# Three edits to a two-layer hybrid encoder trunk: narrow products as columns of the value product, the scatter inside the next item's gate projection, the dense down projection by pairs of blocks

## The reference, cut to what matters

```
FOX_COLS = (FOX_W, FOX_W, FOX_W, FOX_HEADS)                       # 256, 256, 256, 4
DSA_COLS = (DSA_W, DSA_KV_RANK, IDX_HEADS * IDX_HEAD_DIM, IDX_HEAD_DIM, IDX_HEADS)  # 256, 128, 256, 32, 8

rel = relu(einsum('bqhd,bkd->bqhk', qi, k_idx))                   # the one key serves all 8 indexer heads
score = einsum('bqhk,bqh->bqk', rel, wi) * idx_scale

def swiglu(h, w_gate, w_up, w_down):
    return (silu(h @ w_gate) * (h @ w_up)) @ w_down

y = zeros_like(h)                                                 # layer 1: experts
for e in range(N_EXPERTS):
    y = y + gates[..., e:e + 1] * swiglu(h, w_gate[e], w_up[e], w_down[e])
x = x + y
```

## Time and profile before

| what | us |
|---|---|
| three runs: median | 1974.56 |
| lowest, highest | 1971.77, 1974.73 |
| the profiled execution | 1971.14 |
| its span, first to last instruction | 1969.4 |

### The profile page before, as it was taken

One profiled execution on the slowest core, in us unless ns is written; L12 is line 12 of the kernel. 1 busy time (PEld: TensorE's weight loads), 2 busy tenths in 40 slices (PEclk: granted clock), 3 DMA queues, 4 the chain that ended last, 5 costly groups with the idle time before them and its releaser, 6 DMA issues.

```text
span 1969.4 us, 42199 instructions
## 1 busy us (share of the span) xinstructions
PE 1889.3 (96%) x19476; PEld 1260.9 (64%) x19476; DVE 360.0 (18%) x757; ACT 261.4 (13%) x502; POOL 54.1 (3%) x108
## 2 busy tenths in 40 slices
PE   7999999999998999999799999999999999999996
PEld 6887888788887887888635446354453534545364
DVE  1256223100001356223300101001010010100102
ACT  1224111100001324111100000000001000010001
POOL 2100200000000000200000000000000000000000
PEclk9999999999999999999699999999999999999998
DMA  6432212443434332112699999999999999999970
GB/s 182 139 139 86 85 47 86 171 157 142 141 106 136 123 129 86 66 66 86 278 339 366 379 368 393 350 369 363 364 399 362 364 359 361 391 372 374 354 285 23
DMA packets 120758, 462.08 MB, mean 235 GB/s; under 512 B 7486, under 2 KB 18416, under 8 KB 104208
## 3 DMA queue, kind: packets, MB, share of 16 engines
q1 hardware_dynamic: 120592, 459.46, 62.0%
HBM read 458.39 MB, written 1.05 MB: 233 GB/s over the span
## 4 chain that ended last, share of the span: by engine, by line
PE 95%; DVE 2%; ACT 1%; issue 1%; DMA 1%; SPq 0%; DVEq 0%; ACTq 0%
PE bank L989 29%; PE bank L381 25%; PE bank L1013 15%; PE bank L892 4%; PE bank L682 3%; PE bank L852 3%; PE bank L963 2%; PE bank L723 2%; PE bank L839 1%; PE bank L1063 1%; PE bank L1000 1%; PE bank L394 1%; PE bank L367 1%; DMA slot<-in_ffn_w_gate 0%; PE bank L766 0%
## 5 line engine op out<-in xcount | busy, mean ns | idle before, releaser
L989 PE MATMUL bank<-slot,xg 128*32 128x512 f32 (+1 forms) x6144 | 580.6, 539 | 0.7 <-DVE xg L2090 0.7
L381 PE MATMUL bank<-h,slot 128*128 128x256 f32 x2176 | 486.5, 383 | 6.5 <-ACT rel L1442 4.4
L381 PEld LDWEIGHTS bank<-h,slot 128*128 128x128 f32 x2176 | 413.8, 192 | 69.6 <-issue 12.7
L989 PEld LDWEIGHTS bank<-slot,xg 128*32 128x32 f32 x6144 | 207.8, 110 | 367.1 <-issue 355.4
L1013 PE MATMUL bank<-slot,aT 128*32 128x256 f32 x5376 | 295.2, 379 | 0.0
L1013 PEld LDWEIGHTS bank<-slot,aT 128*32 128x32 f32 x5376 | 177.6, 110 | 110.1 <-issue 4.0
L2103 DVE TENSOR_TENSOR av<-gs,bank 128x512 f32<-128x512 f32 (+1 forms) x48 | 29.8, 621 | 703.7 <-PE bank L989 703.7
L892 PE MATMUL bank<-hid,slot 128*128 128x256 f32 x352 | 77.4, 380 | 5.2 <-DVE hid L1979 5.2
L892 PEld LDWEIGHTS bank<-hid,slot 128*128 128x128 f32 x352 | 66.4, 190 | 16.3 <-issue 7.5
L1581 ACT ACTIVATE gs<-bank 128x512 f32<-128x512 f32 (+1 forms) x48 | 25.3, 543 | 284.6 <-PE bank L989 284.5
L1587 ACT ACTIVATE aT<-bank 128x512 f32<-128x512 f32 (+1 forms) x48 | 23.2, 543 | 289.1 <-PE bank L1000 289.1
(11 more groups left out here) (399 smaller groups left out, 1211.3 us busy)
## 6 DMA issues: line engine op xcount, KB each, us to landing
slot<-in_moe_w_gate SPq DMA_DIRECT2D x32, 2048.0 KB, 12.2
slot<-in_moe_w_up SPq DMA_DIRECT2D x32, 2048.0 KB, 12.9
slot<-in_moe_w_down SPq DMA_DIRECT2D x32, 2048.0 KB, 10.2
slot<-in_moe_w_gate SPq DMA_DIRECT2D x32, 1536.0 KB, 7.9
slot<-in_moe_w_up SPq DMA_DIRECT2D x32, 1536.0 KB, 10.9
slot<-in_moe_w_down SPq DMA_DIRECT2D x32, 1536.0 KB, 8.5
slot<-in_w_in SPq DMA_DIRECT2D x20, 2048.0 KB, 8.1
slot<-in_ffn_w_gate SPq DMA_DIRECT2D x5, 2048.0 KB, 7.9
```

What stands on the lines that cost most here:

```text
L381: ins = mm(o, w[:, k, c:c + n], rhs[:, k, :], start=k == 0, stop=k == nk - 1)
L989: ins = mm(banks[b0 + g][32 * p:32 * p + 32, 0:width], xg[:, k, 32 * g:32 * g + 32], w[:, kk, p * width:(p + 1) * width], start=k == 0, st ...
```

## The change

Three edits are made together.

1. The 4 forget columns, the 32 indexer key columns and the 8 indexer weight columns are loaded behind the 256 value columns (`w1` is 300 wide, filled by two DMAs), and one token-major product per half of the tokens makes all of them. ScalarE spreads them with four small copies per half: `ftok`, `iktok`, `iw`, `fv`. After `cc`, PE transposes `ftok` and `iktok` (two 128x128 transposes each) into the places of `ff` and `ik`. POOL's `wf` and `wrep` go, as do the products on them and the 8-column product.
2. In `dense` the down product runs over pairs: both blocks of pair 0 for all eight output blocks, then pair 1. In the last block three `down_part` signals let VectorE add a bank as soon as it is complete.
3. The scatter of an item moves into the next item's gate projection, between its second and third load, and uses the banks 3, 4, 5 and 7 (`SCAT`). The gather and the `Sp` transposes move to the item's end. The first item scatters zeros that POOL wrote; the last item's scatter stands behind the loop.

```diff
+SCAT = (3, 4, 5, 7)
...
+                w = c3(open_slot(pe, L + "w1"), KD, 300)
+                need(pe, "w_tok", 16 * (l + 1))
+                for tt in range(NT):
+                    b = open_bank(pe, f"{l}fv{tt}")
+                    for k in range(KD):
+                        ins = mm(b[:, 0:300], h[:, k, tt * P:(tt + 1) * P], w[:, k, :], start=k == 0, stop=k == KD - 1)
+                    close_bank(ins, f"{l}fv{tt}")
+                free_slot(L + "w1", L + "fv1")
                 b = v2(open_bank(pe, L + "cc"))
...
+                for tt in range(NT):
+                    need_sb(pe, f"{l}fv{tt}")
+                for nm, src in (("ff", ftok), ("ik", iktok)):
+                    b = v4(open_bank(pe, L + nm))
+                    for tt in range(NT):
+                        ins = nc.tensor.transpose(b[:, tt, :], src[:, tt, :], ident[:, :])
+                    close_bank(ins, L + nm)
                 pair(L + "dq", wn, 0)
...
-                        for m in range(KD):
-                            for k in range(nf):
-                                ins = mm(v2(banks[4 + m // 2])[:, m % 2, :], w[:, k, m * P:(m + 1) * P],
-                                         hid[:, k, :], start=first and k == 0, stop=last and k == nf - 1,
-                                         skip_group_check=True)
+                            for m in range(KD):
+                                for k in range(2 * g, 2 * g + 2):
+                                    ins = mm(v2(banks[4 + m // 2])[:, m % 2, :], w[:, k, m * P:(m + 1) * P],
+                                             hid[:, k, :], start=first and k == 0, stop=last and k == nf - 1,
+                                             skip_group_check=True)
+                                if last and m % 2 and m < KD - 1:
+                                    ins.then_inc(S["down_part"], 1)
...
+                def scatter_add():
+                    pe.wait_ge(S["spt_done"], i * 2 + 2)
+                    pe.wait_ge(S["ys_act"], i + 1)
+                    pe.wait_ge(S["ys_dve"], i + 1)
+                    scatter()
...
                     for q in range(4):
+                        if q == 2 and between is not None:
+                            between()
...
                 def gate_bank(g):
                     if g == 0:
+                        pe.wait_ge(S["xg_done"], i * 2 + 1)
+                    elif g == 1:
                         pe.wait_ge(S["xg_done"], i * 2 + 2)
-                    elif g == 2:
-                        pe.wait_ge(S["x_done"], i * 4 + 1)
+                    else:
+                        pe.wait_ge(S["spt_done"], i * 2 + 1)
...
+                sp.dma_start(w[:, :, 0:260], wv[:, :, FOX0 + 512:FOX0 + 772]).then_inc(slot_full[s], 16)
+                sp.dma_start(w[:, :, 260:300], wv[:, :, DSA0 + 640:DSA0 + 680]).then_inc(S["w_tok"], 16)
...
+                for tt in range(NT):
+                    b = take(act, f"{l}fv{tt}")
+                    fcol = ftok[:, tt, :].rearrange("p (u c) -> p u c", u=2)[:, :, 0:4]
+                    step(copy(fcol, b[:, 256:260].unsqueeze(1).broadcast_to([P, 2, 4])))
+                    step(copy(iktok[:, tt, :].rearrange("p (r c) -> p r c", r=4),
+                              b[:, 260:292].unsqueeze(1).broadcast_to([P, 4, 32])))
+                    step(copy(iw[:, tt, :], b[:, 292:300], 1 / 16))
+                    done(copy(fv[:, tt, :], b[:, 0:256]), f"{l}fv{tt}")
...
+            need(gp, "x_ready", 4)
+            nc.gpsimd.memset(Ys[:, :, :], 0.0).then_inc(S["ys_act"], 1)
+            nc.gpsimd.memset(SpT[:, :, :], 0.0).then_inc(S["spt_done"], 2)
+            nc.gpsimd.memset(cst[:, 0:1], 0.0).then_inc(S["ys_dve"], 1)
```

More of the change, by code:

```diff
@@ L965, in gather, with scatter @@
                     ins.then_inc(S["xg_full"], 1)
+            def scatter():
+                for j in range(2):
+                    for g in range(NG):
+                        for p in range(4):
+                            ins = mm(v2(banks[SCAT[p]])[:, j, :], Ys[32 * p:32 * p + 32, g, j * P:(j + 1) * P],
+                                     SpT[32 * p:32 * p + 32, g, :], start=g == 0, stop=g == NG - 1)
+                            if j == 1 and g == NG - 1:
+                                ins.then_inc(S["s_full"], 1)
             pe.wait_ge(S["sel_item"], 1)
@@ L1009, in down @@
                             pe.wait_ge(S["aT_done"], i * 6 + (3 * half + g + 1))
+                            if half == 0 and g == 2:
+                                pe.wait_ge(S["x_done"], i * 4 + 4)
                         o = banks[7][:, 0:256] if g == 2 else banks[6][:, 256 * g:256 * g + 256]
@@ L1069, in _ @@
             nc.switch_bb("item_end")
+            pe.wait_ge(S["spt_done"], items * 2 + 2)
+            pe.wait_ge(S["ys_act"], items + 1)
+            pe.wait_ge(S["ys_dve"], items + 1)
+            scatter()
             n = 2 * DEPTH
@@ L1412, in _ @@
                 evac(L + "fk", fk[:, :, :], v2)
-                evac(L + "fv", fv[:, :, :], v2)
+                need(act, "f_w", 1)
+                for tt in range(NT):
+                    b = take(act, f"{l}fv{tt}")
[5 more added lines that the diff above has]
+                    done(copy(fv[:, tt, :], b[:, 0:256]), f"{l}fv{tt}")
+                b = take(act, L + "cc")
+                step(A(cc[:, :], b[:, 0:T], ACT.Copy))
+                A(ccs[:, :], b[:, 0:T], ACT.Square, scale=KV ** -0.5).then_inc(S["css"], 1)
+                done(A(junk[:, :], cst[:, 4:5], ACT.Copy), L + "cc")
                 b = take(act, L + "ff")
@@ L2092, in _, with add_item @@
             slots4 = iota[:, 0:CAP].rearrange("p (g c) -> p g c", c=32).unsqueeze(2).broadcast_to([P, NG, 4, 32])
+            def add_item(i):
+                for p in range(4):
+                    dve.wait_ge(S["s_full"], i * 4 + (p + 1))
+                    o = x[:, 2 * p:2 * p + 2, :]
+                    tt_(o, o, v2(banks[SCAT[p]]), ALU.add).then_inc(S["x_done"], 1)
             with dve.Fori(0, items) as i:
@@ L2118, in _ @@
                 V.tensor_copy(Ys[:, 2, :], banks[7][:, 0:256]).then_inc(S["ys_dve"], 1)
-                for p in range(4):
-                    dve.wait_ge(S["s_full"], i * 4 + (p + 1))
-                    o = x[:, 2 * p:2 * p + 2, :]
-                    tt_(o, o, v2(banks[2 + p]), ALU.add).then_inc(S["x_done"], 1)
+            add_item(items)
             dve.wait_ge(S["x_done"], items * 4 + 4)
```

116 lines of the change are left out of this document (36 added, 80 removed).

## The result

| | before | changed |
|---|---|---|
| median, us | 1974.64 (4 runs) | 1941.39 (4 runs) |
| lowest, highest | 1971.77, 1979.91 | 1940.98, 1942.36 |
| profiled execution, its span | 1971.14, 1969.4 | 1940.98, 1939.2 |

The ratio is 0.983 (95% interval 0.981 to 0.985): 1.7% faster. Between the profiled executions it is 30.2 us of span, where the sum gave 26.1; the rest of the distance to the forecast of 1947.5 is the start from the profile. The time lies at the range's lower edge, 1941; the ratio times the forecast's starting point, 0.9829 x 1974.56, gives 1940.8, just outside it. A second set of four runs of the changed kernel had a median of 1942.88 (1941.05 to 1943.17), ratio 0.985 (0.983 to 0.987).

The account below looks back on a forecast made before the run. TensorE (PE), 95% of the chain, was taken to bound the kernel. Savings of 18.3 + 6.1 + 1.7 = 26.1 us from the profiled 1971.14 gave 1945.0; from the runs' ends 1945.7 and 1948.6, so 1947.5 was taken, range 1941 to 1956.

Parts of the forecast that it names:

- A: Narrow products, both layers: 8.74 us less PE work plus 0.4 from the clock per layer, 18.3 us saved.
- B: Dense down product: 4.35 us of hid waits and 1.75 us at the norm go, 6.1 us saved.
- C: Expert loop: Ys waits -5.1, first item -0.65, zero scatter +2.87, exit waits +1.2; -1.7 us in all.
- Rival 1: Expert stage bound by its loads: removed waits return as slot waits, 23.2 us saved, 1950; chance 0.06.
- rival 2: Narrow-product saving mostly given back, by PE idle behind rel (1966) or 300 columns costing like 512 (1962); chance 0.08.
- the clock under `css` and `ql`: Full-width products ahead of css speed up this stretch: 0.4 us a layer taken, with ends 0 and 0.8.
- second half-clock stretch: At the product behind rel, after PE's wait (81 us): the 1.2 GHz stretch was said to stay.
- 5 x 0.87 = 4.35 us: Five full dense blocks: each loses its 0.87 us wait for hid, since pair 0's products cover pair 1.
- I take zero: Dense down product: switching output groups every two products was put at no change in cost.
- Both levels of the runs: Whole kernel: the range was to cover both ends of the runs before, from which the sum gave 1945.7 and 1948.6.
- Rival 3: Expert loop's branch exposed at all eight turns, 6.1 us each: 23 us slower, 1997; chance 0.03.
- Trainium skill's rule: Loop branch: a taken branch whose target isn't in the fetched window stalls for a DMA fetch of it.

Follow-up runs that it names:

- B alone: The kernel before with only the second edit (dense down product by pairs, down_part signals): 1965.72 us, ratio 0.9956.
- C alone: The kernel before with only the third edit (scatter inside the next item's gate, gather at the item's end): 1974.12 us, ratio 0.9986.
- A alone: The kernel before with only the first edit (300-column value product, transposes, narrow products gone): 1956.61 us, ratio 0.9898.

## Why the prediction was wrong by a little

**Direction and mechanism of all three edits were right; the step that failed is what the sum left out and where it started.** In profiled executions the gain was 30.2 us and not 26.1. The stretches without an edit, put at nothing, gave 3.9. That the edits' own stretches came to 26.3 for 26.1 is luck: A was 0.5 better than its term, B 1.3 better and C 1.5 worse. On top of that I raised 1945.0 to 1947.5, between the ends of the runs, and the 2.5 us were not needed.

Where I wrote numbers for TensorE's own instructions they held: 8.08 us for 8.10, 0.44 for 0.44, an item's wait of 0.64 for `Ys` gone, the wait at the exit 1.07 for 1.2, the norm 1.76 for 1.75, no wait for slots or copies. Rival 1 (the loads) and rival 2 (A given back) didn't come; TensorE waited for no slot, and its idle time ahead of `r0` went from 2.34 to 2.67 us.

**"A = 2 x (8.74 + 0.4) = 18.3 us"** measured 9.49 and 9.27, 18.8. The mis-sized part is the clock under `css` and `ql`, 0.73 in layer 0 and 0.50 in layer 1 for 0.4; the run with the 8-column product put back showed 1.5 us in layer 1, `css` included, and 0.8 in layer 0. The second half-clock stretch, behind `rel`, stayed, as said.

**"5 x 0.87 = 4.35 us"** is the mis-sized term of B; by the traces it is 5.6. The four full periods between the down products shrank by 1.11 us each. I had counted the wait and set the product behind it at no change ("I take zero"), but a down product that starts behind an idle engine took 14.05 us and one that doesn't 13.81. The runs with both waits ahead and with B alone show the two values, with and without the wait.

**"C = -1.7 us"** measured 0.2 in the first profile and 2.4 in the second. The terms hold: seven periods 0.76 us shorter (I had 0.64) and the zero scatter 2.80 us. What the sum lacked is a gap of 1.21 us at the loop's exit, which is a draw, and the first gather: it should have fallen by 0.65 us to the first gate matmul and grew from 6.35 to 6.98, at 1.2 GHz for longer. That is a draw as well; C alone took 5.88 and A alone 7.79.

**Nothing was set down for places that the change doesn't touch**, and 3.9 us came from there. 1.6 at `w_lora` and 1.4 of the 2.2 between recurrence and gather were half-clock stretches that the profiled execution of before had drawn and that of the changed kernel had not. The other 0.8 of the 2.2 is time in the recurrence that goes with edit A; why is open. The sum was made against one execution, and I allowed the other places no draw. "Both levels of the runs" were taken for two levels 3 us apart; 60 runs of before lie between 1965.6 and 1980.8.

**Rival 3** was the right fear, and its price came out by luck. Unhinted, a turn loses 6.5 us (I had put 6.1, half of a load's 12.2, a time for data and not for code), seven turns pay and not eight, and 46 us in all make the kernel slower than before. Of the Trainium skill's rule ("Runtime: NRT & Kernel Launch", instruction fetch mechanics) I wrote that the loop as it stood should then show a stall. That was too quick: the rule and the row agree, because the hint hides the fetch, and only for a hint that stands far enough ahead. 8.4 us were enough, 3.7 and 4 were not. The chance of 0.03 rested on the time behind the hint, 8.4 us for 7.5, and that argument was sound.

## What to carry to other kernels

Take a wait out and the product behind it can get cheaper too (13.81 for 14.05 us here). Narrow products ahead of a chain can bring a lower clock onto it, so price an edit with the row at the clock that it will meet. A hint for a branch has to stand further ahead than the fetch takes (here 8.4 us were enough and 4 were not, where an unhinted turn lost 4.2 to 4.5), so whoever moves work across it should measure the turn again. Compare stretches between the same two instructions in several executions: the sum of all stretches carries draws of 1.5 to 3 us each, as large as a small edit.

## What the runs showed that I had not expected

- A hint for the loop's branch is worth 46 us in 1940; one 4 us ahead gave nothing (gaps of 4.8 to 5.1 us against 4.2 to 4.5 without one, in a loop of another form), one 3.7 us ahead about 1 us a turn.
- The place of a loop's code, moved by 128 instructions, cost 1.06 us a turn, with no change in data or waits, and the profile puts it down to a copy that was long over. C alone, whose loop stands further along still, pays nothing. Whether the hint is 8.4 or 16 us ahead makes no difference to it. The mechanism is open.
- 32 instructions of 8 columns (3.47 us) ahead of a chain cost another 0.8 and 1.5 us in it, at 1.2 GHz. The product itself took 3.47 us in most traces and 4.45 in C alone, so the kernel with it also varies more.
- The half-clock stretches fall at other places from one execution to the next: the first pair took 3.69 us in seven of the sixteen profiled executions and 5.2 to 6.7 in nine, and both in the changed kernel.
